# A two-block model on one core: the opening written in another order, and the distance table stored by one repeating DMA

## The reference

```python
c_act = jax.nn.silu(c)
mod = c_act @ w_ada[l] + b_ada[l]                      # 6 x 1024 values
sh1, sc1, g1, sh2, sc2, g2 = split(mod, 6)
h = _rmsnorm(x, norm_attn_g[l]) * (1.0 + sc1) + sh1    # x: 512 tokens x 1024
proj = h @ w_in[l]
...
bias = rel_bias[_t5_bucket(distance)]                  # per head, a function of the distance alone
s = q @ k.T * dh ** -0.5 + bias
```

## Time and profile before

| | us |
|---|---|
| runs of the kernel before (median, lowest, highest of 3) | 4019.6, 4018.7, 4020.7 |
| the profiled execution's own time | 4020.7 |
| its span, first to last instruction | 4018.6 |
| TensorE busy, share of the span | 3687.0, 92% |
| DVE busy | 2240.2, 56% |
| ACT busy | 1055.1, 26% |
| first instruction to the first norm tile (DVE L2149) | 87.95 |

### The profile page before, as it was taken

How to read it: one execution, slowest core, us unless ns; L and a number is a source line. 1 busy time by engine, 2 the same in 40 slices (tenths; PEclk the granted TensorE clock), 3 DMA queues, 4 the chain that set the end, 5 groups by cost and what they waited for, 6 DMA issues and landing times. The chain is left out here.

```text
span 4018.6 us, 47579 instructions
## 1 busy us (share of the span) xinstructions
PE 3687.0 (92%) x19172; PEld 2994.5 (75%) x19172; DVE 2240.2 (56%) x5186; ACT 1055.1 (26%) x1633; POOL 215.5 (5%) x189
## 2 busy tenths in 40 slices
PE   6889998999889999877889999998999997789998
PEld 3755886788778888765448888887888885457886
DVE  5564556755666666745345666676666534434334
ACT  3354002322331211233242212123212123233222
POOL 1012101000000000100000000010000010000000
PEclk9998887999989999988989999998999998899999
DMA  5532003444323333333102333332333323012332
GB/s 161 152 99 71 1 1 84 114 121 118 105 74 98 102 100 105 91 96 97 46 16 84 95 105 95 111 98 81 95 106 95 96 53 90 27 42 84 94 95 68
DMA packets 663804, 348.35 MB, mean 87 GB/s; under 512 B 29989, under 2 KB 658919, under 8 KB 663328
## 3 DMA queue, kind: packets, MB, share of 16 engines
q1 hardware_dynamic: 662432, 342.69, 30.3%
q10 hardware_dynamic: 1152, 2.62, 0.2%
HBM read 340.55 MB, written 4.72 MB: 86 GB/s over the span
## 5 line engine op out<-in xcount | busy, mean ns | idle before, releaser
L1736 PE MATMUL psum<-hn_high,high 128*128 128x512 f32 (+2 forms) x3360 | 1225.2, 365 | 74.9 <-DVE low L2123 53.7
L1738 PE MATMUL psum<-hn_high,low 128*128 128x512 f32 (+2 forms) x3360 | 1201.6, 358 | 0.0
L1737 PE MATMUL psum<-hn_low,high 128*128 128x512 f32 (+2 forms) x3360 | 1201.1, 357 | 0.0
L1736 PEld LDWEIGHTS psum<-hn_high,high 128*128 128x128 f32 (+1 forms) x3360 | 639.6, 190 | 197.9 <-DVE hn_low L2154 35.3
L1738 PEld LDWEIGHTS psum<-hn_high,low 128*128 128x128 f32 (+1 forms) x3360 | 638.4, 190 | 101.2 <-issue 0.9
L1737 PEld LDWEIGHTS psum<-hn_low,high 128*128 128x128 f32 (+1 forms) x3360 | 640.3, 191 | 91.5 <-issue 0.5
L2123 DVE TENSOR_TENSOR low<-stage,high 128x1024 fp32r<-128x1024 f32 (+3 forms) x440 | 524.6, 1212 | 190.2 <-ACT high L1442 189.6
L2179 DVE SCALAR_TENSOR_TENSOR partial<-stage,cond,partial 128x128 f32<-128x128 f32 x2304 | 625.5, 349 | 0.0
L1442 ACT ACTIVATE high<-stage 128x1024 fp32r<-128x1024 f32 (+3 forms) x440 | 437.6, 1017 | 506.5 <-DMA stage<-in_w_ffn 364.8
L1736 PE MATMUL psum<-hidden_high,high 128*128 128x512 f32 (+1 forms) x1408 | 499.1, 354 | 4.0 <-DVE low L2123 4.0
L1738 PE MATMUL psum<-hidden_high,low 128*128 128x512 f32 (+1 forms) x1408 | 492.3, 350 | 0.0
(11 more groups left out here) (299 smaller groups left out, 3151.6 us busy)
## 6 DMA issues: line engine op xcount, KB each, us to landing
stage<-in_w_ffn SPq DMA_DIRECT2D x240, 512.0 KB, 4.6
stage<-in_w_ada SPq DMA_DIRECT2D x192, 512.0 KB, 4.0
stage<-in_w_in SPq DMA_DIRECT2D x56, 512.0 KB, 5.2
stage<-in_w_out SPq DMA_DIRECT2D x32, 512.0 KB, 4.3
stage<-in_w_ffn SPq DMA_DIRECT2D x32, 384.0 KB, 4.0
stage<-in_w_gate SPq DMA_DIRECT2D x22, 512.0 KB, 4.0
stage<-in_w_up SPq DMA_DIRECT2D x22, 512.0 KB, 5.2
stage<-in_w_down SPq DMA_DIRECT2D x16, 512.0 KB, 4.2
```

The source lines that it names most:

```text
L1736: self.e.matmul(out, high[:, i], xh, start=first and i == 0, stop=False)
L1737: self.e.matmul(out, high[:, i], xl, start=False, stop=False)
L1738: done = self.e.matmul(out, low[:, i], xh, start=False, stop=last and i == nk - 1)
```

## The change

Only the opening and what belongs to it is written anew.

- SP's first call (`load_first`) issues `eye` and the 6 rows of tile 0 (with the condition vector `c`), then the planner asks for four `w_ada` blocks, and only then come the tokens, the context and the four small vectors.
- The 19 rows of tiles 1 and 2 are issued from ACT's queue, under one semaphore (`rows_landed`).
- The transposes of the rows are split: tile 0 first, with the condition `c` alone; tiles 1 and 2 and the other two conditions in step 5.
- The distance table is made in step 2, for all heads by one product of 8 output rows (`relb` itself is the weight). `rel_wide` is gone. ACT copies 8 rows of 640 and issues a single DMA, whose source repeats each row 128 times.
- Main tile k is turned in step 6 + k, context tile k in step 8 + k; `residual_root` is called in step 14, and its result handed to `modulated_norm`.

The diff, cut to its core:

```diff
-        self.rel_wide = self.area("rel_wide", HEADS1 * P)[0:N_BUCKETS + 1].rearrange("p (h n) -> p h n", n=P)
-        self.distances = [self.area("distances", SKEW) for _ in range(2)]
+        self.distances = self.area("distances", SKEW)[0:HEADS1]
...
     def setup(self):
         mem = self.mem
         self.clear()
+        self.load_first()
+        if self.board.plan is not None:
+            self.bring_to(STAGES - 1)
         self.load_start()
-        bank = self.mix.next()
-        self.turn_vectors(bank)
-        bank.free = [("vec",)]
-        for n, name in enumerate(("c", "c2", "c_ctx")):
-            t = self.temps.next()
-            self.condition(n, mem.column(name, KT), t)
-            t.free = [("cond", n)]
+        self.take_vectors(0, 1)
+        self.take_condition(0, "c")
...
     def distance_bias(self):
         self.distance_tables()
-        for h in range(HEADS1):
-            for o, n in ((0, 512), (512, SKEW - 512)):
-                bank = self.mix.next()
-                self.distance_row(h, o, n, bank)
-                bank.free = [("distance", h, o)]
-            self.store_distances(h)
-            yield
+        for o, n in ((0, 512), (512, SKEW - 512)):
+            bank = self.mix.next()
+            self.distance_rows(o, n, bank)
+            bank.free = [("distances", o)]
+        self.store_distances()
...
         for j in range(2 * KT):
             one(j)
-            self.token_jobs[j]()
+            if j == 2:
+                self.distance_bias()
+            if j == 5:
+                self.take_vectors(1, 3)
+                self.take_condition(1, "c2")
+                self.take_condition(2, "c_ctx")
+            if 6 <= j < 6 + KT:
+                self.token_jobs[j - 6]()
             if j >= KT:
-                next(distances)
+                self.token_jobs[j]()
+            if j == 2 * KT - 2:
+                root = self.residual_root(main, "norm_attn")
...
+    def load_first(self):
+        self.dma(self.misc(), ("eye",), self.mem.eye[:], self.mem.const["eye"])
+        self.wait_ge("cleared")
+        for n, (tile, dst, src) in enumerate(self.mem.rows):
+            if tile == 0:
+                self.dma(self.misc(), ("row", n), dst, src)
...
+    def distance_rows(self, o, n, bank):
+        self.wait_ge("distance_sums", o)
+        self.e.activation(self.mem.distances[:, o:o + n], bank.ap[0:HEADS1, 0:n], ACT.Copy).then_inc(*self.mark("distances", o))
+
+    def store_distances(self):
+
+        self.wait_ge("distances", 512)
+        self.dma("skew_landed", ("skewed",), self.mem.skew.rearrange("h (p n) -> h p n", p=P),
+                 self.mem.distances.rearrange("h (o n) -> h o n", o=1).broadcast_to([HEADS1, P, SKEW]))
```

More of the change, by code:

```diff
@@ L221, in put @@
             n = ap.shape[0]
-            self.rows.append((self.vectors[row:row + n, tile, 0:ap.shape[1]], ap))
+            self.rows.append((tile, self.vectors[row:row + n, tile, 0:ap.shape[1]], ap))
             self.col[name] = (tile, row)
@@ L598, in residual_root, with modulated_norm @@
         return bank.ap[:, 0:part.T], ("inverse", name), bank
-    def modulated_norm(self, name, part, gain, shift, after):
+    def modulated_norm(self, name, part, gain, shift, after, root=None):
         T = part.T
         self.bring_two()
-        rinv, ready, t = self.residual_root(part, name)
+        rinv, ready, t = root or self.residual_root(part, name)
         high, low = part.hn
@@ L681, in setup, with take_vectors, take_condition @@
             self.token_jobs += [lambda k=k, part=part, x=x: self.token_job(k, part, x) for k in range(KT)]
+    def take_vectors(self, lo, hi):
+        bank = self.mix.next()
+        self.turn_vectors(bank, lo, hi)
+        bank.free = [("vec", lo)]
+    def take_condition(self, n, name):
+        t = self.temps.next()
+        self.condition(n, self.mem.column(name, KT), t, ("vec", 0 if n == 0 else 1))
+        t.free = [("cond", n)]
     def token_job(self, k, part, x):
@@ L775, in first_block @@
         self.gains("norm_attn", mem.gain[:, :, 0], vec(1), mem.column("norm_attn", KT), first_two)
-        self.modulated_norm("norm_attn", main, mem.gain[:, :, 0:1], vec(0), [("gain", "norm_attn"), *first_two])
+        self.modulated_norm("norm_attn", main, mem.gain[:, :, 0:1], vec(0), [("gain", "norm_attn"), *first_two], root=root)
         self.clear_pads()
@@ L1298 @@
 class Sync(Walk):
+    def load_first(self):
[4 more added lines that the diff above has]
+                self.dma(self.misc(), ("row", n), dst, src)
     def load_start(self):
         mem, i = self.mem, self.mem.inp
[L1303 to L1306, removed]
         col = lambda ap: ap.rearrange("(n o) -> n o", o=1)
+        self.dma(self.misc(), ("tokens", "main"), mem.tokens_main, i["x"][0].rearrange("(a p) n -> p a n", p=P))
+        self.dma(self.misc(), ("tokens", "ctx"), mem.tokens_ctx, i["ctx_2"][0].rearrange("(a p) n -> p a n", p=P))
         self.dma(self.misc(), ("small", 0), mem.dt_bias, col(i["dt_bias"][0]))
@@ L1388, in distance_tables @@
         self.e.memset(mem.relb, 1.0).then_inc(*self.mark("one"))
[L1389 to L1392, removed]
     def conv(self, f, ps, done, acc):
@@ L1473, in norm_tile, with condition @@
         self.e.activation(high, xs, ACT.Identity, bias=shift).then_inc(*self.mark("norm_high", name, k))
-    def condition(self, n, x, t):
-        self.wait_ge("vec")
+    def condition(self, n, x, t, ready):
+        self.wait_ge(*ready)
         self.wait_free(t)
@@ L1482, in turn_tokens, with load_start @@
         self.e.activation(part.h[:, k, :], bank.ap[:, 0:part.T], ACT.Copy).then_inc(*self.mark("tokens_in", part.name, k))
[L1484 to L1494, removed]
+    def load_start(self):
+        self.wait_ge("cleared")
+        for n, (tile, dst, src) in enumerate(self.mem.rows):
+            if tile:
+                self.dma_counts["rows_landed"] = self.dma_counts.get("rows_landed", 0) + 16
+                self.e.dma_start(dst, src).then_inc(self.sems["rows_landed"], 16)
+        self.board.new["late_rows",] = "rows_landed", self.dma_counts["rows_landed"]
+    def distance_rows(self, o, n, bank):
[5 more added lines that the diff above has]
+                 self.mem.distances.rearrange("h (o n) -> h o n", o=1).broadcast_to([HEADS1, P, SKEW]))
     def gate_row(self, name, ps, done):
@@ L1772, in modulation_vector, with turn_vectors @@
         done.then_inc(*self.mark("mod_psum", name))
-    def turn_vectors(self, bank):
+    def turn_vectors(self, bank, lo, hi):
         mem = self.mem
-        for n in range(len(mem.rows)):
-            self.wait_ge("row", n)
+        if lo:
+            self.wait_ge("late_rows")
+        else:
+            for n, (tile, _, _) in enumerate(mem.rows):
+                if tile == 0:
+                    self.wait_ge("row", n)
         self.wait_ge("eye")
         self.wait_ge("ones")
-        for a in range(3):
+        self.wait_free(bank)
+        for a in range(lo, hi):
             done = self.e.transpose(bank.ap[:, a * P:(a + 1) * P], mem.vectors[:, a, :], mem.eye[:])
-        done.then_inc(*self.mark("vec_turned"))
+        done.then_inc(*self.mark("vec_turned", lo))
     def turn_tokens(self, k, part, x, bank):
@@ L1789, in turn_tokens, with distance_rows @@
         done.then_inc(*self.mark("tokens_turned", part.name, k))
-    def distance_row(self, h, o, n, bank):
+    def distance_rows(self, o, n, bank):
         mem = self.mem
-        self.wait_ge("rel_wide")
+        self.wait_ge("one")
+        self.wait_ge("rel_bias")
         self.wait_ge("distance_table")
         self.wait_free(bank)
-        self.e.matmul(bank.ap[:, 0:n], mem.rel_wide[:, h, :], mem.table[:, o:o + n], start=True, stop=True) \
-            .then_inc(*self.mark("distance_sum", h, o))
+        self.e.matmul(bank.ap[0:HEADS1, 0:n], mem.relb, mem.table[:, o:o + n], start=True, stop=True) \
+            .then_inc(*self.mark("distance_sums", o))
     def gate_rows(self, bank):
@@ L2540, in build @@
         mem = Memory(nc, ctx, inp, const, out)
-        landed = [f"{n}_landed" for n in ("out", "skew0", "skew1", *(f"stage{i}" for i in range(STAGES)),
+        landed = [f"{n}_landed" for n in ("out", "skew", "rows", *(f"stage{i}" for i in range(STAGES)),
                                          *(f"misc{i}" for i in range(MISC)))]
```

20 lines of the change are left out of this document (9 added, 11 removed).

## The result

The changed kernel takes **4040.1 us** (median of 6 runs, 4038.3 to 4040.8), the kernel before 4020.0 in the same comparison: a ratio of 1.005, 95% interval 1.0039 to 1.006. It is 20 us slower. The profiled execution has a span of 4038.1 us, 19.5 more than before. The forecast was 4039.

The account below looks back on a forecast made before the run. The opening was taken to be bound by `w_ada` blocks waiting for the narrow store: block 9 at 79.5, vectors to 90.9, then 6.5 and 9.7 us, norm at 107.1 against 87.95, 19.2 us later, 4039 us; range 4002 to 4048.

Parts of the forecast that it names:

- Only the opening counts: Before the first norm tile at 87.95 us: every microsecond won or lost there passes one for one into the time.
- The front: Opening's start: condition there and DVE starting at about 9.6 us, 15.1 earlier; a wait on the products until 25.1.
- The store: Distance store of 2.62 MB from 8 partitions: 50 GB/s, 52 us, from 26.5 to 78.5; 46 to 61 us had 0.60.
- The turns: DMA queues during the store: a block gets at most one packet turn per store packet, so two blocks pass at best.
- Block 8 comes after half of the store, at 53.5: `w_ada` block 8, waiting beside the store, lands at 53.5 us; block 9 lands with the store's end, 79.5.
- From block 9 to the norm: End of the opening: vectors 9 to 12 and three additions until 90.9 us, then 6.5 and 9.7 us, norm at 107.1.
- The chain: After vector 12's sums, at the last main tile: vector sum, transposes, square, addition, sum over partitions, 6.5 us.
- the tail: Last stretch before the norm: two sums, table load wait, spreading, last vector sums, context tile, gain and halves, 9.7 us.
- Rival 1: Store on eight engines at full speed, 14 us, 18 with turns: norm at 72.9, 4005 us; chance 0.29, including 0.06 for 3998.
- Rival 2: Store at half engine speed, 28 us: norm at 83, 5 us gained, 4015; chance 0.09 with what lies around break-even.
- The break-even: Store of 33 us, 79 GB/s: block 9 lands at 60.3 and the norm stays at 87.95; a slower store loses.
- the ends of the bound: Store duration extremes: 13.6 us if eight engines run at full speed, 110 us if speed goes with partitions (4096, chance 0.02).

Follow-up runs that it names:

- tables_first: The changed kernel with its store from 128 source partitions, plus loads of the distance table and `rel_bias` moved ahead of the first `w_ada` block: 3999.9 us, ratio 0.9953.

## Why the prediction was right

**Only the opening counts.** If every microsecond at the norm is passed on, span minus norm is a constant. It is 3930.7 before, 3929.7 after, and between 3927.0 and 3930.7 in ten of the eleven experiments. The exception is the late store, 3966.1, which moves a wait behind the norm.

**The front.** First sums at 9.62, said 9.6 (SP issued 30 small loads before the tokens, not the 29 of the prediction, which is 0.2 us on ACT's 19). DVE goes on at 26.27, said 25.1: the products start at 23.01 instead of 21.8.

**The store.** Said: 50 GB/s, 52 us. Measured: 49 GB/s, packets of 395 ns, so 128 of them on each of eight engines are 51 us. I came to 50 from one row of tiles of 16 and 8 partitions, and the size was right, in part by luck: in that 1.1 us the engines also moved 239 packets of a block, and the tile's width changed. I scaled by the number of partitions; the table above shows that their place counts, since eight rows on 0, 4, .. 28 flow at 178 GB/s. The Trainium skill, "SBUF — State Buffer", section "Door 1: The DMA port swizzle", states 27.2 GB/s for each of 16 ports and puts partitions 0 to 7 on two of them, by which the store would last 48 us, an estimate. All four narrow stores agree with its map of partitions to ports, and it is from this map that I take groups of four, since the runs alone would allow groups of eight; where ports are the limit, in the first three rows of the table, the rate is 24.5 GB/s a port, a tenth below its figure. Its 16 ports have a meaning for the choice of rows, too: the map gives 0, 4, .. 28 eight different ports.

**The turns.** Said: at most a turn for each of the store's, block 8 after half of it, at 53.5, block 9 with its end, at 79.5. The turns are there, 400 packets to 402 in 21 us. But **"Block 8 comes after half of the store, at 53.5"** failed: it came at 71.6. Two things were missing. Block 8 was not yet in the queue when the store began: its buffer comes free with the sums of vector 4, which stood behind the products, so it was issued at 28.48. That is 1 to 2 us. The larger one is that the turns do not start at once: from about 27 us to between 42 and 44 the engines of the store took no packet of a block, some 37 to 42 packets each (q1 moves 1 packet from 42 to 43 us, 8 in the next microsecond and 16 in the one after it). From there 64 turns of 0.395 + 0.027 us are 27 us more, so the last engine is done near 71; the block was read at 71.6. The end hardly noticed, since block 9 decides, which the end of the store releases: 82.1 for 79.5. The clause that block 8 too might come at the end of the store, with 2 us more, was the nearer one in its time, but not in its reason, since the turns were one for one.

**From block 9 to the norm.** The sums of vector 12 end at 89.68 + 3.73 = 93.4, said 90.9: that is block 9's 2.6 us and nothing more, since four vectors and the additions on them took 11.3 us, said 11.4. The chain then took 6.6 (to 100.03), said 6.5, and the tail 8.4, said 9.7. Norm at 108.4, said 107.1. That the time came within 1.1 us of the forecast is again partly luck: block 9 came 2.6 us later than said, and the tail was 1.3 us shorter.

**The rivals.** Rival 1, engines at full speed, came true with other partitions: its 4005 stands against 4002.3 with the rows spread. Rival 2, a store of 28 us and 4015, is what four groups gave: 26 us and 4015.5 and 4015.7. The break-even, a store of 33 us, was near: at 26 us the change gains 4, at 51 it loses 20, and a line between the two crosses zero near 31, an estimate. So the prediction turned on one number, which nothing in the profile before showed directly. The chance of 0.60 for it seems fair in hindsight: the section of the Trainium skill named above spoke for it, one row pointed that way, and the ends of the bound lay at 4005 and 4096.

## What to carry to other kernels

A DMA that repeats a few rows saves compute, but it reads them through the ways in that these rows have: before using one, count the groups of four partitions on the SBUF side and take 24 GB/s for each, as measured here on partitions 0 to 15 (whether groups farther apart, such as 0 to 3 and 32 to 35, are ways of their own no run here tests); widen the source (here a product with 128 output rows took 2.50 us, the one with 8 rows 2.29) or spread it. Then ask what else is on the same DMA engines: a slow store does not only end late, it holds up every load behind it, by far more than its bytes. And a wait that is removed can let a transfer start earlier, as in `tables_first`, where the norm came no earlier; in the same step, move that transfer to where the DMA engines are idle.

## What the runs showed that I had not expected

- **A head start, but not everywhere.** In the change the store's engines serve it alone for 37 to 42 packets each and only then take turns: none of q1's from 37 to 41 us. With sixteen rows there is none from 32 to 42, and with 128 rows there are 16 to 749 in the 5 us from 28 on. But in the old order with 128 rows, where the store is issued at 55.95, the turns are already there from 60 to 65 us:

```profile
q10 hardware_dynamic: 653, 1.67, 83.3%
q1 hardware_dynamic: 658, 0.34, 22.2%
```

  So its length is no constant of a store, and what sets it stays open. It is the step that the prediction lacked, and the least understood one here.
- **Turns go by packets, not by bytes or time.** A block's packet of 512 bytes takes 0.032 x 16 x 21 / 400 = 27 ns, the store's 395, and they alternate. On the eight shared engines the block gets a sixteenth of the time.
- **SP stands still.** With two blocks waiting, the issue of the third took 31.95 us. Any small load behind it on that queue would have stood there too.
- **A fast store holds loads up as well.** 128 rows at 384 GB/s take 102% of 16 engines as the profile counts, or 83% where a block takes turns with them (the lines above). So it matters where even a fast store stands: with it at 17.67 us DVE waited 9.1 us for blocks in its first 130, with it at 40.20 3.5.
